# Hybrid attention block on one core: bias additions, norm chain, weight sums and last evictions at other places of the attention order

## The chip, the core and the metric

The kernel runs on one core of a Trainium2 chip. Five engines run their own in-order instruction queues: TensorE (PE; PEld are its weight loads), VectorE (DVE), ScalarE (ACT), GpSimd (POOL) and SyncE (SP), which here only issues DMAs. ACT issues DMAs too. They wait for one another by semaphores alone. The metric is the device time of one execution in microseconds; the median of several runs counts.

## The reference

All in float32, one layer, a sequence of 2048 tokens of width 1024:

```
h = rms_norm(x);  [q | k | v | p] = h @ w_in            (512 | 128 | 128 | 512 columns)
a = sliding_window_sink_attention(rms_norm(q), rms_norm(k), v)   8 heads, 2 KV heads, window 128
m = multiscale_pool(p)          trailing means over 2, 4, 8, 16 tokens minus the token, a map per group, bias, scale
x = x + concat([a, m]) @ w_out
x = x + (silu(gate) * val) @ w_down     gate | val = causal conv(3) of rms_norm(x) @ w_up, 2 * 2816 columns
```

## The kernel before

The sequence is cut into four blocks `a` of 512 tokens, each of four tiles of 128. A float32 product is made of three passes on PE over halves of the numbers: `passes` multiplies high by high, high by low and low by high (lines 1037 to 1039; a 128x512 matmul starts every 0.227 us). The high half of a weight is a copy on ACT (`split`, line 1419, into `w_hi`), the low half a subtraction on DVE (line 1899, into `w_lo`); halves once made for block 0 are kept in DRAM and brought back by SP (`bring`, lines 775 and 776). Weights move in units of 512 KB, through a ring of three; SP and the splits run two units (`LEAD`) ahead of PE.

The attention part, some 480 us, goes by one list, written out by hand in `attention_order()`: each entry is a step and a block. Every engine walks the same list (`walk`) and does its own share of each step, in that order; what it has no share in, it passes over. So the place of an entry orders an engine's own queue, and semaphores order the engines. Steps that the change touches, with their shares:

- `n1sq`, `n1sc` (a): norm of x. ACT squares four tiles, POOL takes the root, DVE multiplies by it (`n1sc`, line 1910, four instructions). `t1` then turns the tiles on PE (line 1109), with ACT making `hT_hi` and DVE `hT_lo` (line 1944) out of each bank; from the fifth tile on PE waits for the `hT_lo` that frees the bank.
- `pin` (a, g): the pooling projections, 24 long matmuls each; ACT carries them out of PSUM (lines 1486 to 1489), `win` on DVE makes the trailing sums (lines 1959, 1968).
- `q` (a, k): q's projection. In the last of four units ACT squares, DVE sums (2086), POOL takes the root (2505, 2507), DVE scales (2091), tile by tile.
- `s` (a, t): scores on PE (1214), two tiles to a pair of banks; DVE takes the maxima (2174), ACT the exponentials (1592). `inv` on DVE adds the sink to `row_sum` (line 2157, 128x8) and inverts it (2160); POOL multiplies the probabilities by it (2554). `sp`, `pt`, `av` spread, copy and multiply them by v.
- `o` (a, h, k) and, for blocks 1 and 2, `w`, `tp`, `tb`: the output projection; DVE adds the result to x (`r` or `n`; lines 2007 and 2023, the evictions). For blocks 1 and 2 it is a Winograd-like form with fewer products, on sums of weights made once in block 1: `to_load` (SP, lines 862, 863), `to_sum` (DVE, 2048), `to_hi` (ACT, 1579), `to_lo` (DVE, 2052), `to_store` (SP), j = 0 to 3.
- `bias_load`, `bias_sum`, `bias`: the folded bias, made once. `r_load` (SP, line 812) then brings x of block 0 into `r`, which `bias_sum` used. `rb` (b) adds the bias to block b's four tiles on POOL (line 2581); for blocks 0 and 1 it waits for each tile's last eviction.
- `n2sq`, `n2sc` (b): the second norm. ACT stores x2 by DMA (line 1638) and squares it (1440), after `rb`; DVE scales (1910) once all four stores have landed, since it writes over them; `t2` turns the tiles on PE (1337).

The mixer of block a-1 (`o`, `w`, `rb`, `n2sq`) runs inside the list's part for block a. Behind the attention part come the up-projection and the down-projection, on PE all the time.

Of the kernel before, what the change touches and what calls it, by code (L numbers as in the profile page):

```python
# [32 lines left out]
RAW, RING, LEAD, KEEP = 2, 3, 2, 4  # L33
# [3 lines left out]
def attention_order():  # L37
# [13 lines left out]
    for a in range(NB):  # L51
# [17 lines left out]
        units("q", a, (1,))  # L69
        if a == 1:  # L70
            units("r_load", a, ())
        if not more:
            units("rb", a - 1, ())
        units("win", a, (3,))
        if more:
            units("n1sc", a + 1, ())
        if a > 1:
            units("halves", a - 1, (2,))
        units("q", a, (2,))
        if a == 1:  # L80
            units("bias", a, ())
            units("to_sum", a, (0,))
        if not back:
# [42 lines left out]
        if a == 1:  # L126
            units("to_load", a, (0,))
            units("to_hi", a, (0,))
# [13 lines left out]
            units("o", a - 1, (1, 0))  # L142
            units("inv", a, (0,))
            units("o", a - 1, (1, 1))
            units("to_store", a, (0,))
            units("s", a, (2,), (3,))
            units("join", a, (0,), (1,))
            units("o", a - 1, (1, 2), (1, 3))
            units("to_store", a, (1,), (2,))
            units("inv", a, (1,))  # L150
        else:
# [28 lines left out]
            units("join", a, (1,))  # L180
            units("w", a - 1, (6, 1))
            units("inv", a, (1,))
        if more:
            units("rb", a - 1, ())
        if more:
# [5 lines left out]
            units("pin", a + 1, (0,))  # L191
            units("win", a + 1, (0,))
            if a == 1:
                units("to_sum", a, (3,))
            units("av", a, (0,), (1,))
            if a == 1:
                units("to_hi", a, (3,))
            units("n2sq", a - 1, ())
            units("pin", a + 1, (1,))
            if a == 1:  # L200
                units("to_load", a, (3,))
                units("to_lo", a, (3,))
            units("win", a + 1, (1,))
            units("n2sc", a - 1, ())
            units("sp", a, (2,), (3,))
# [46 lines left out]
UNIT = {}  # L252
# [184 lines left out]
def bass_hybrid_block(nc, x, norm1_g, w_in, q_norm_g, k_norm_g, attn_sinks, pool_w, pool_b, pool_scale,  # L437
# [20 lines left out]
    with ExitStack() as ctx:  # L458
# [576 lines left out]
        def _(pe):  # L1035
# [76 lines left out]
            def pin(a, n, g):  # L1112
# [12 lines left out]
                for i, k in enumerate(t1_order(a)):  # L1125
                    if g == 0 and i > (0, -1, 4, 4)[a]:
                        pe.wait_ge(S["hT_lo"], KT * a + i + 1)
                    if (a, g) == (1, 0) and i + 2 < KT:
                        turn_tile(a, i + 2)
                    c = slice(k * P, (k + 1) * P)  # L1130
                    mm = passes(ps[:, P_BANK + g, :], w_hi[:, w, c], w_lo[:, w, c], hT_hi[:, k, :], hT_lo[:, k, :],
                                i == 0, i == KT - 1)
# [70 lines left out]

            def s(a, t):
                pe.wait_ge(S["kT_ready"], a + 1)
                pe.wait_ge(S["qT_ready"], NT * a + (2, 4, 4, 4)[t])
# [683 lines left out]
        def _(dve):  # L1890
# [135 lines left out]
            def w(b, n, i, k):  # L2026
                if i == 6:
                    split(n + LEAD)
                if k == 1:
                    added(b, i, 0)  # L2030
                    added(b, i, 1)

            def swl(b, k):
# [62 lines left out]
            def q(a, n, k):  # L2096
                split(n + LEAD)
                if k < 3 or a == 0:
                    return
                for t in range(NT):  # L2100
                    summed(a, t)
                    if t == 2 and a - 1 in SEVEN:
                        split(UNIT["w", a - 1, 1, 0])
                    if t:
                        scaled(a, t - 1)
                if a - 1 in SEVEN:
                    split(UNIT["w", a - 1, 1, 1])
                scaled(a, NT - 1)
# [554 lines left out]
```

## Time and profile before

| | |
|---|---|
| runs, us | 1764.26 median of 3 (1764.02 to 1765.81) |
| the profiled execution, us | 1765.85; its span, first to last instruction, 1764.1 |
| busy us of the span | PE 1748.3, DVE 1340.5, ACT 822.2, POOL 302.0 |
| mean granted TensorE clock | 0.999 of full speed |
| DMA | 201 GB/s over the span |

The page tells busy time of each engine; a view of waits tells who stood idle and which engine's result ended it; a timeline lists one engine's instructions in order, in square brackets the idle time before one and what ended it. Ends of matmuls are modelled: of PE the distance between starts says more than a duration.

### The profile page before, as it was taken

Reading aid. Unit: us, or ns where it says so; the run is one execution under the profiler, and the core shown is the slowest. Engines: PE = TensorE matmul, PEld = TensorE weight load, DVE = VectorE, ACT = ScalarE, POOL = GpSimd, SP = SyncE. Lnnn points to the kernel's source line nnn. Section 1 sums busy time; section 2 is a strip of 40 time slices with the busy share of each in tenths; the row PEclk is TensorE's granted clock in tenths of the full one; section 3 lists DMA queues with packets and bytes.
Section 4 is the critical chain, followed back from the end, with each engine's and each line's share of the span. In section 5 each row is a group of like instructions: output and inputs, shape, how many; then the busy total and the mean of one; then the engine's idle time right before and its main releaser. Section 6 shows DMA issues by size and latency. Waiting matters only on the chain.

```text
span 1764.1 us, 23493 instructions
## 1 busy us (share of the span) xinstructions
PE 1748.3 (99%) x8454; PEld 1454.6 (82%) x8454; DVE 1340.5 (76%) x1773; ACT 822.2 (47%) x1448; POOL 302.0 (17%) x296
## 2 busy tenths in 40 slices
PE   8999999999999999999999999999999999999999
PEld 7787888888888888888888888888888888888887
DVE  4656856566789888889888878878877778865874
ACT  4565645535665444444454444444444433333321
POOL 2353312434110000000000000000004023220210
PEclk9999999999999999999999999999999999999999
DMA  8867688577747433332375232232237998976883
GB/s 325 282 226 281 237 323 297 206 286 263 252 154 259 136 95 120 132 95 72 132 279 174 84 96 72 84 91 77 79 95 242 345 354 316 306 254 222 293 287 131
DMA packets 224245, 355.30 MB, mean 201 GB/s; under 512 B 14650, under 2 KB 107010, under 8 KB 223106
## 3 DMA queue, kind: packets, MB, share of 16 engines
q1 hardware_dynamic: 204702, 301.31, 50.5%
q10 hardware_dynamic: 19427, 52.49, 7.6%
q8 instruction: 68, 1.11, 0.3%
q14 instruction: 48, 0.39, 0.1%
HBM read 273.00 MB, written 80.74 MB: 201 GB/s over the span
## 4 chain that ended last, share of the span: by engine, by line
PE 92%; DVE 3%; DMA 1%; ACT 1%; POOL 1%; issue 1%; SPq 0%; ACTq 0%; DVEq 0%
PE ps L1037 30%; PE ps L1039 29%; PE ps L1038 29%; DVE sums L1959 1%; PE ps L1214 1%; PE ps L1337 1%; POOL ss_q L2507 1%; PE ps L1238 1%; PE ps L1225 1%; DMA wP_d<-wp_kept 0%; DVE w_lo L1899 0%; PE ps L1109 0%; DMA raw<-in_w_in_dram 0%; DMA raw<-in_w_out_dram 0%; PE ps L1201 0%
## 5 line engine op out<-in xcount | busy, mean ns | idle before, releaser
L1037 PE MATMUL ps<-va_hi,wv 128*128 128x512 f32 x1232 | 479.4, 389 | 0.0
L1039 PE MATMUL ps<-va_hi,wv 128*128 128x512 f32 x1232 | 479.3, 389 | 0.0
L1038 PE MATMUL ps<-va_lo,wv 128*128 128x512 f32 x1232 | 479.3, 389 | 0.0
L1039 PEld LDWEIGHTS ps<-va_hi,wv 128*128 128x128 f32 x1232 | 231.3, 188 | 48.0
L1037 PEld LDWEIGHTS ps<-va_hi,wv 128*128 128x128 f32 x1232 | 231.3, 188 | 47.9
L1038 PEld LDWEIGHTS ps<-va_lo,wv 128*128 128x128 f32 x1232 | 231.3, 188 | 47.8
L1037 PE MATMUL ps<-dt_hi,ds_hi 128*128 128x512 f32 x616 | 239.6, 389 | 0.0
L1038 PE MATMUL ps<-dt_lo,ds_hi 128*128 128x512 f32 x616 | 239.6, 389 | 0.0
L1039 PE MATMUL ps<-dt_hi,ds_lo 128*128 128x512 f32 x616 | 239.6, 389 | 0.0
L2311 DVE SCALAR_TENSOR_TENSOR cb<-ub,cst,cb 128x1024 f32<-128x1024 f32 x176 | 217.8, 1279 | 8.3 <-ACT cb L1736 8.3
L1736 ACT ACTIVATE cb<-ub,cst 128x1024 f32<-128x1024 f32 x88 | 109.2, 1244 | 158.2 <-DVE ub L2360 94.5
L1853 ACT ACTIVATE ds_hi<-dts 128x512 fp32r<-128x512 f32 x110 | 69.5, 632 | 153.5 <-PE ps L1039 115.7
L1038 PEld LDWEIGHTS ps<-dt_lo,ds_hi 128*128 128x128 f32 x616 | 115.7, 188 | 24.1
L1037 PEld LDWEIGHTS ps<-dt_hi,ds_hi 128*128 128x128 f32 x616 | 115.7, 188 | 24.0
L1039 PEld LDWEIGHTS ps<-dt_hi,ds_lo 128*128 128x128 f32 x616 | 115.7, 188 | 23.9
L2631 POOL TENSOR_TENSOR dtw<-dw 128x512 f32<-128x512 f32 x55 | 86.7, 1578 | 276.9 <-DMA dw<-in_w_down_dram 250.0
L1688 ACT ACTIVATE wv<-tt 128x512 fp32r<-128x512 f32 x168 | 100.3, 623 | 65.2 <-PE ps L1039 40.3
L2464 DVE TENSOR_TENSOR ds_lo<-dts,ds_hi 128x512 fp32r<-128x512 f32 x110 | 91.4, 831 | 37.6 <-ACT ds_hi L1853 37.3
L2218 DVE TENSOR_TENSOR wv<-tt,wv 128x512 fp32r<-128x512 f32 x168 | 111.7, 686 | 4.0
L1688 ACT ACTIVATE wv<-rw 128x512 fp32r<-128x512 f32 x126 | 78.3, 623 | 57.7 <-DVE cb L2316 51.2
L2459 DVE TENSOR_TENSOR dts<-dg 128x512 f32<-128x512 f32 x110 | 80.1, 728 | 27.5 <-DMA dg<-gT_d 27.3
L1742 ACT ACTIVATE ub<-cb 128x1024 f32<-128x1024 f32 x44 | 46.8, 1063 | 98.8 <-DVE cb L2311 98.8
(223 smaller groups left out, 2894.0 us busy)
## 6 DMA issues: line engine op xcount, KB each, us to landing
dg<-gT_d SPq DMA_DIRECT2D x264, 256.0 KB, 5.4
rw<-in_w_up_dram SPq DMA_DIRECT2D x84, 512.0 KB, 5.2
dw<-in_w_down_dram SPq DMA_DIRECT2D x132, 256.0 KB, 5.5
gT_d<-cb ACTq DMA_DIRECT2D x44, 512.0 KB, 2.6
w_hi<-wA_d SPq DMA_DIRECT2D x30, 512.0 KB, 4.2
w_lo<-wA_d SPq DMA_DIRECT2D x30, 512.0 KB, 6.2
n<-in_x_dram SPq DMA_DIRECT2D x16, 512.0 KB, 8.6
raw<-in_w_out_dram SPq DMA_DIRECT2D x16, 512.0 KB, 5.0
```

What stands on the lines that cost most here:

```text
L1037: pe.matmul(out_ap, l_hi, r_hi, start=first, stop=False, skip_group_check=True)
L1038: pe.matmul(out_ap, l_hi, r_lo, start=False, stop=False, skip_group_check=True)
L1039: return pe.matmul(out_ap, l_lo, r_hi, start=False, stop=last, skip_group_check=True)
L1688: a_.activation(wv_hi[:, wslot(un, i), :], w_source(i), ACT.Copy).then_inc(S["u_hi"], 1)
L1736: a_.activation(cb[:, s, :], ub[:, s, 2:], ACT.Identity, bias=cbias[:, col], scale=cw[2][:, col]).then_inc(S[("tap2g", "tap2v")[s]], 1)
L1742: a_.activation(ub[:, 0, 2:], cb[:, 0, :], ACT.Silu).then_inc(S["silu"], 1)
L1853: a_.activation(ds_hi[:, sigma % SSLOTS, :], s_source(sigma), ACT.Copy).then_inc(S["s_hi"], 1)
L2218: v.tensor_tensor(wv_lo[:, w, :], w_source(i), as_f32(wv_hi[:, w, :]), ALU.subtract).then_inc(S["u_lo"], 1)
L2311: v.scalar_tensor_tensor(cb[:, s, :], ub[:, s, j:j + TS], cw[j][:, col], cb[:, s, :], ALU.mult, ALU.add).then_inc(S["conv"], 1)
L2459: v.tensor_tensor(s_source(sigma), dg[sigma % GRAW][:, 0, :], dg[sigma % GRAW][:, 1, :], ALU.subtract if minus else ALU.add).then_inc(S["s ...
L2464: v.tensor_tensor(ds_lo[:, sigma % SSLOTS, :], s_source(sigma), as_f32(ds_hi[:, sigma % SSLOTS, :]), ALU.subtract).then_inc(S["s_lo"], 1)
L2631: g_.tensor_tensor(t_source(tau), dw[:, tau % WRAW, 0, :], dw[:, tau % WRAW, 1, :], ALU.subtract if minus else ALU.add).then_inc(S["t_adde ...
```

## The change

Moves in the order (the first five points), and three edits in the programs of PE and DVE:

- `r_load(1)` goes from behind (q, 1, 1) to behind (q, 1, 3).
- `to_sum(1, 0)` goes ahead of (q, 1, 2), into the place of `n1sc(2)`, and `to_load(1, 0)` ahead of (q, 1, 3); `n1sc(2)` goes behind `inv(1, 0)`.
- `rb(0)` goes from behind `inv(1, 1)` to ahead of it, `rb(1)` likewise ahead of `inv(2, 1)`.
- In block 1, `to_sum(1, 3)` goes behind `av`, and `to_hi(1, 3)` behind `n2sq(0)`.
- `n2sc` goes ahead of `win(a+1, 1)`, in blocks 1 and 2, and in block 1 ahead of `to_lo(1, 3)`.
- PE: the scores (0, 3) are issued after two of the eight steps of unit (pin, 1, 3).
- DVE: in `w` the two evictions go ahead of the split; in `q` the split of (w, a-1, 1, 1) goes ahead of the third scaling.

```diff
--- before.py
+++ after.py
@@ -67,19 +67,19 @@
         if a > 1:
             units("halves", a - 1, (1,))
         units("q", a, (1,))
-        if a == 1:
-            units("r_load", a, ())
         if not more:
             units("rb", a - 1, ())
         units("win", a, (3,))
-        if more:
+        if a == 1:
+            units("to_sum", a, (0,))
+        elif more:
             units("n1sc", a + 1, ())
         if a > 1:
             units("halves", a - 1, (2,))
         units("q", a, (2,))
         if a == 1:
+            units("to_load", a, (0,))
             units("bias", a, ())
-            units("to_sum", a, (0,))
         if not back:
             units("wp", a, (0, 0))
         units("q", a, (3,))
@@ -124,7 +124,7 @@
             units("kve", a + 1, ())
             continue
         if a == 1:
-            units("to_load", a, (0,))
+            units("r_load", a, ())
             units("to_hi", a, (0,))
             units("o", a - 1, (0, 0), (0, 1))
             units("to_lo", a, (0,))
@@ -141,12 +141,14 @@
             units("to_lo", a, (1,), (2,))
             units("o", a - 1, (1, 0))
             units("inv", a, (0,))
+            units("n1sc", a + 1, ())
             units("o", a - 1, (1, 1))
             units("to_store", a, (0,))
             units("s", a, (2,), (3,))
             units("join", a, (0,), (1,))
             units("o", a - 1, (1, 2), (1, 3))
             units("to_store", a, (1,), (2,))
+            units("rb", a - 1, ())
             units("inv", a, (1,))
         else:
             units("w", a - 1, (0, 0), (0, 1), (1, 0))
@@ -179,9 +181,9 @@
             units("w", a - 1, (6, 0))
             units("join", a, (1,))
             units("w", a - 1, (6, 1))
+            if more:
+                units("rb", a - 1, ())
             units("inv", a, (1,))
-        if more:
-            units("rb", a - 1, ())
         if more:
             units("t1", a + 1, (0,))
             units("sp", a, (0,))
@@ -190,18 +192,18 @@
             units("pt", a, (0,), (1,))
             units("pin", a + 1, (0,))
             units("win", a + 1, (0,))
+            units("av", a, (0,), (1,))
+            units("n2sq", a - 1, ())
             if a == 1:
                 units("to_sum", a, (3,))
-            units("av", a, (0,), (1,))
-            if a == 1:
                 units("to_hi", a, (3,))
-            units("n2sq", a - 1, ())
             units("pin", a + 1, (1,))
             if a == 1:
                 units("to_load", a, (3,))
+            units("n2sc", a - 1, ())
+            if a == 1:
                 units("to_lo", a, (3,))
             units("win", a + 1, (1,))
-            units("n2sc", a - 1, ())
             units("sp", a, (2,), (3,))
             units("pt", a, (2,), (3,))
             units("pin", a + 1, (2,))
@@ -1125,6 +1127,8 @@
                 for i, k in enumerate(t1_order(a)):
                     if g == 0 and i > (0, -1, 4, 4)[a]:
                         pe.wait_ge(S["hT_lo"], KT * a + i + 1)
+                    if (a, g, i) == (1, 3, 2):
+                        scores(0, 3)
                     if (a, g) == (1, 0) and i + 2 < KT:
                         turn_tile(a, i + 2)
                     c = slice(k * P, (k + 1) * P)
@@ -1202,6 +1206,10 @@
                     mm.then_inc(S["qT_done"], 1)
 
             def s(a, t):
+                if (a, t) != (0, 3):
+                    scores(a, t)
+
+            def scores(a, t):
                 pe.wait_ge(S["kT_ready"], a + 1)
                 pe.wait_ge(S["qT_ready"], NT * a + (2, 4, 4, 4)[t])
                 if t >= 2:
@@ -2024,11 +2032,11 @@
                                 ).then_inc(S["out_added"], 1)
 
             def w(b, n, i, k):
-                if i == 6:
-                    split(n + LEAD)
                 if k == 1:
                     added(b, i, 0)
                     added(b, i, 1)
+                if i == 6:
+                    split(n + LEAD)
 
             def swl(b, k):
                 split(UNIT["w", b, 6, k])
@@ -2101,10 +2109,10 @@
                     summed(a, t)
                     if t == 2 and a - 1 in SEVEN:
                         split(UNIT["w", a - 1, 1, 0])
+                    if t == 3 and a - 1 in SEVEN:
+                        split(UNIT["w", a - 1, 1, 1])
                     if t:
                         scaled(a, t - 1)
-                if a - 1 in SEVEN:
-                    split(UNIT["w", a - 1, 1, 1])
                 scaled(a, NT - 1)
 
             def qn(a):
```

## Rows read from the trace of the kernel before

**Rows 1.** The page, its part 1: busy us, share of the span, instructions.
```profile
PE 1748.3 (99%) x8454; PEld 1454.6 (82%) x8454; DVE 1340.5 (76%) x1773; ACT 822.2 (47%) x1448; POOL 302.0 (17%) x296
```

**Rows 2.** PE's waits from 15 to 480 us: in total, times, longest.
```profile
PE ps L1337 <- DVE r L1910: 2.1, 1, 2.1
PE ps L1037 <- DVE w_lo L1899: 2.0, 2, 1.9
...
PE ps L1037 <- DVE n L2023: 0.5, 1, 0.5
PE ps L1214 <- ACT xs L1592: 0.5, 1, 0.5
PE ps L1225 <- DVE cat_lo L2195: 0.5, 1, 0.5
PE ps L1037 <- DMA w_lo<-wA_d: 0.4, 1, 0.4
```

**Rows 3.** Timeline of PE: start, us, line, out<-in, xcount [idle before <-releaser].
```profile
102.69 1.16 PE L1214 MATMUL ps<-kT,qT 64*128 64x128 f32 x16 [0.50 <-ACT xs L1592]
```

**Rows 4.** Timeline of SP's queue, 128 to 143 us.
```profile
128.89 0.43 SPq L812 DMA_DIRECT2D r<-in_x_dram  x1
```

**Rows 5.** DMA issues, KB, us to landing: from 128.87, 131.5 and 120.5 us.
```profile
r<-in_x_dram SPq DMA_DIRECT2D x1, 2048.0 KB, 11.2
...
w_lo<-wA_d SPq DMA_DIRECT2D x1, 512.0 KB, 10.9
...
wP_d<-wp_kept ACTq DMA_DIRECT2D x2, 256.0 KB, 6.5
```

**Rows 6.** Timeline of DVE, 149 to 169 us.
```profile
149.71 2.74 DVE L1910 TENSOR_SCALAR n<-n,rstd 128x1024 f32<-128x1024 f32 x4
...
156.27 1.22 DVE L1899 TENSOR_TENSOR w_lo<-raw,w_hi 128x1024 fp32r<-128x1024 f32 x1
157.41 1.27 DVE L2086 TENSOR_REDUCE ss_q<-xs 128x8 f32<-128x512 f32 x2
...
166.77 2.35 DVE L1899 TENSOR_TENSOR w_lo<-raw,w_hi 128x1024 fp32r<-128x1024 f32 x2
```

**Rows 7.** Timeline of PE at 168 us.
```profile
168.13 0.47 PE L1037 MATMUL ps<-w_hi,cat_hi 128*128 128x512 f32 x1 [1.85 <-DVE w_lo L1899]
```

**Rows 8.** Timeline of DVE, 192 to 213 us.
```profile
194.22 2.87 DVE L1899 TENSOR_TENSOR w_lo<-raw,w_hi 128x1024 fp32r<-128x1024 f32 x1
...
207.29 0.69 DVE L2007 TENSOR_TENSOR r<-ps,r 128x512 f32<-128x512 f32 x1 [0.67 <-PE ps L1039]
...
208.53 4.70 DVE L1944 SCALAR_TENSOR_TENSOR hT_lo<-ps,cst,hT_hi 128x512 fp32r<-128x512 f32 x7
```

**Rows 9.** Timeline of POOL, 193 to 222 us.
```profile
194.12 4.73 POOL L2554 TENSOR_TENSOR xs<-xs,row_sum 128x1024 f32<-128x1024 f32 x2 [27.99 <-DVE row_sum L2160]
208.37 3.76 POOL L2554 TENSOR_TENSOR xs<-xs,row_sum 128x1024 f32<-128x1024 f32 x2 [9.52 <-DVE row_sum L2160]
212.08 9.44 POOL L2581 TENSOR_TENSOR r<-r,bias_all 128x1024 f32<-128x1024 f32 x4
```

**Rows 10.** Timeline of DVE at 109 us and at 382 us.
```profile
109.83 0.95 DVE L2157 TENSOR_TENSOR row_sum<-row_sum,sink_exp 128x8 f32<-128x8 f32 x1 [1.05 <-ACT xs L1592]
...
381.79 5.60 DVE L1959 TENSOR_TENSOR sums<-sums 128x525 f32<-128x525 f32 x2
```

**Rows 11.** Timeline of PE at 210 us and at 238 us.
```profile
209.71 2.26 PE L1109 MATMUL ps<-ident,n 128*128 128x128 f32 x16
...
237.89 1.72 PE L1337 MATMUL ps<-ident,r 128*128 128x128 f32 x8 [2.06 <-DVE r L1910]
```

**Rows 12.** Windows: stretch, its us, busy (x) PE PEld DVE ACT POOL, clock, DMA.
```profile
239.00:240.00 1.00, 1.00 (x5) 0.90 (x4) 1.00 (x1) 0.83 (x2) 0.00 (x0) 0.50 1.03 422
```

**Rows 13.** Timeline of DVE at 329 us.
```profile
328.93 0.75 DVE L1944 SCALAR_TENSOR_TENSOR hT_lo<-ps,cst,hT_hi 128x512 fp32r<-128x512 f32 x1
```

**Rows 14.** Timeline of PE at 331 us.
```profile
330.70 1.95 PE L1109 MATMUL ps<-ident,n 128*128 128x128 f32 x16
```

## Prediction

> **What bounds the kernel now.** I read the page first. TensorE (PE) is busy in 99% of the span [rows 1], so no engine can be made faster to any use: all that is to be had, or lost, is the time in which PE stands still. The view of PE's waits from 15 to 480 us, the attention part, holds nearly all of it [rows 2]: 2.1 us for `n2sc` of block 0, 2.0 us (1.9 of it one wait) for a weight's low half `w_lo`, and four waits of about half a microsecond: for an exponential (ACT xs), for a DMA of `w_lo`, for `cat_lo`, and for an eviction into `n`. After 480 us PE shows no stall worth a line, so the change can move the end only by moving PE at these places or by making a new one. Most moves of this diff are on DVE, POOL and SP, each an in-order queue, so each has to be followed to the next thing that PE waits for. The timelines of these queues give the rest. Times below are positions in the trace of before.
>
> **1. Block 0's last scores.** PE has to wait 0.50 us before the scores of tile 3, at 102.69, until the exponentials of tile 1 have left the bank [rows 3]. With six of unit (pin, 1, 3)'s 24 matmuls between them (24 take 5.4 us, so six about 1.4) the wait is covered. With the restart it makes 0.7 us; one more change between small and long matmuls, there and back, takes an estimated 0.4 of it back (those around this row leave PE some 0.2 each). Gain 0.3 us (bounds 0 and 0.5). DVE sees tile 3's scores 0.7 us later, but ACT is still at tile 2's exponentials then.
>
> **2. r_load.** It issues 2 MB at 128.89, in front of the halves of unit (q, 1, 2), and takes 11.2 us to land; those halves take 10.9 us and PE stands 0.44 us for them [rows 2, 4, 5]. Behind the halves it is gone from their way: gain 0.65 us with PE's restart (bounds 0.5 and 0.7). What it is moved past matters too: it now stands on SP's queue just ahead of the loads of units (o, 0, 0, 0) and (o, 0, 0, 1), whose splits gate step 3.
>
> **3. Weight sums of block 1.** PE's 1.85 us stand before 168.13 ends with `w_lo` of (o, 0, 0, 2) [rows 7]. Read back on DVE [rows 6]: that split (166.77) comes after four rounds of q's norm chain, which began at 157.41; from that beginning to PE's restart are 10.7 us, all of them a chain. The chain began when DVE had done `n1sc` (2.74 us), a split, `to_sum` and the second split (1.22, at 156.27). Now `n1sc` is gone from there, and `to_sum` runs earlier, because `to_load` is issued before the load of (q, 1, 3). Then DVE is no longer last; the raw weights of (o, 0, 0, 1) are. `to_load` waits for the stores of wP_d: 6.5 us to land in a like place [rows 5], so about 138.2. Behind it on the queue come 1 MB of sums, 1 MB of halves, 2 MB of r and 1 MB of raw weights; at 1.35 us per 512 KB (the two halves of (q, 1, 2) land in the 2.7 us behind r: 131.91 + 10.9 against 128.89 + 11.2) the last lands 13.5 us on, and with some 1.5 us until the first moves at about 153, and with ACT's and DVE's halves of the split (1.1 and 1.2) the chain starts at 155.3 instead of 157.4. PE reaches that point 2.1 us earlier than before, steps 1 and 2 included. Bounds: 1.1 (the queue is a microsecond slower) and 2.9 (PE itself is late).
>
> **4. n1sc(2) behind inv(1, 0).** These four DVE instructions (2.74 us) now stand in front of the split of (o, 0, 1, 3), beside POOL's two multiplications at 194.12, 4.73 us for both, 1.9 each where nothing is beside them [rows 8, 9]. The split that stands there took 2.87 us where the same form takes 1.22 [rows 6, 8]: it waited for the first of them to end. The same is seen of a tiny addition (0.95 us instead of 0.16, beside a POOL multiplication) and of window sums beside POOL's bias additions (5.60 us for two that take 0.7 alone): DVE instructions with two SBUF inputs run only between two of POOL's [rows 10]. If `n1sc` waits likewise, its first runs when the first multiplication ends (196.0), the second after the second one (198.6), and the split ends at 201.7 instead of 197.1. If it doesn't, 200. No row shows a TENSOR_SCALAR behind POOL; I take the first, by the row at the very place [rows 8]. Everything of DVE up to the last evictions of o(0, 1) then moves by 4.2 us. The first of these, so far done at 204.97 and with room, ends at 209.1, the last at 211.0 instead of 208.0 [rows 8]. PE wants to turn block 2's tiles into those banks at 207.09 and waits 2 us.
> The Trainium skill (SBUF — State Buffer, Who interferes with whom) says that a `tensor_scalar` in a two-port mode and a GpSimd instruction block each other for the whole instruction, whoever comes first. By that rule `n1sc` waits, as I took it; without it the next step's 5.7 us would be 4.2.
>
> **5. rb(0) ahead of inv(1, 1).** This is the step that costs. The bias additions are 4 x 2.36 us on POOL (9.44, at 212.08) [rows 9]. They now start as soon as tile 0 is evicted, at 209.1, and DVE's `inv` stands right behind the last eviction. It holds two additions of row_sum, both inputs in SBUF, one after the other, with a reciprocal between. By [rows 10] the first waits for the end of the running bias addition (211.5), and, 0.3 us later, the second finds POOL's next one running and waits for its end (213.9). Behind it on DVE stands `hT_lo` of block 2, which began at 208.53 [rows 8] and now ends its first piece at 214.9; PE's second group of transposes (209.71, a tile per bank, each after a piece of `hT_lo`) starts there, and (pin, 2, 0) starts at 218.2 instead of 212.6 (the group's end, the second spread, then the pool unit) [rows 11]. Cost 5.7 us with step 4; 4.2 if `n1sc` doesn't wait. PE is idle for 2.5 us at a stretch in it. Of such a gap the trace has one case each way: after 1.85 us the clock stayed (168.13), after 2.06 us the granted clock was 0.50, the lower of its two levels (1.2 GHz), for some 3 us [rows 7, 11, 12]. I add 1.0 us here (bounds 0 and 1.6).
>
> **6. rb(1) ahead of inv(2, 1).** The same in block 2, without `n1sc`. rb starts at 327.05, after the 13th eviction; inv's additions are let in at 329.5 and 331.9, and `hT_lo` starts at 332.0 instead of 328.93 [rows 13]. PE's group at 330.70 waits for it: 2.9 us [rows 14]. Its gap is 2.0 us, between the two cases above: I add nothing, with 1.5 as the upper bound. That the muls behind rb end later (218 and 340 instead of 212 and 332) costs nothing: the probabilities are wanted 4 us and more after that.
>
> **7. n2sq, n2sc, to_sum(3), to_hi(3), win in block 1.** With rb 7 us earlier and ACT's squares ahead of `to_hi`, `n2sc` can run right after the stores of x2, and `win` after it. Counted from PE's start of (pin, 2, 0), the last store lands about 16.5 us on, `n2sc` is done at 19.4, and PE wants it at 22.3. So the wait of 2.06 us is gone, and the slow clock behind it (1.55 us: eight transposes in 1.72 us, the next matmuls at 0.43 instead of 0.23) [rows 11, 12]. `cat_lo` now precedes `to_sum`: its 0.46 us go too. With the restarts 4.4 us in all (bounds 3.5 and 4.8). Late next is `to_lo(3)` and block 1's `lefts`, with some microseconds of idle DVE behind them. For block 2 `n2sc` comes before `win`: `win` waits, nobody waits for it.
>
> **8. Last evictions of block 2 ahead of the split.** The wait of 0.54 us for `n` sits behind a split, 1.22 us in this form [rows 2, 6]. Gain 0.6 (0.5 to 0.7). The split of (w, a-1, 1, 1) one tile earlier: its ACT half is just ready then, nothing gained or lost.
>
> **Sum.** Gains 2.1 + 4.4 + 0.6 = 7.1; costs 5.7 + 1.0 + 2.9 = 9.6; together +2.5 us. The profiled execution took 1765.85 us, its span 1764.1; with the change 1768.35 and 1766.6. It is 1.6 above the median of the runs, 1764.26; the difference carries over: 1766.8 us. Changes under 0.2%, 3.5 us, are about what can't be told from none.
>
> **Rivals.**
> (a) POOL does not hold DVE's small additions up for long (both slip in at one boundary, or before the first bias addition has begun). Speaks for it: additions of 128x8 need the port for almost nothing. Against it: the addition of 0.95 us is of just this form, and a second instruction 0.03 us after the first found the port taken [rows 10]. If both slip in, step 5 costs 2 and step 6 0.6: 7.1 - 2.6 = 4.5 gained, 1759.8 us; if nothing waits, 7.1 gained, 1757.2.
> (b) Slower: the clock. If the idle stretches of steps 5 and 6 both bring the lower level, as the 2.06 us did, with 1.5 us each, and the SP queue leaves only 1.1 in step 3, then 6.1 gained and 5.7 + 2.9 + 3.0 lost: +5.5, 1769.8 us. It decides from a gap of between 1.85 and 2.06 us, and step 6's is 2.0.
> (c) r only changes what waits: the raw weights come behind it, step 3 gives nothing but steps 1 and 2, and (o, 0, 0, 0) itself is late; the rest as forecast: +3.6, 1767.9 us. It is an end of the forecast's range.
>
> **Chances.** Forecast with (c) 0.55, (a) 0.22, (b) 0.23. The forecast's own range is 1764 to 1769 (n1sc without waits -1.5, step 3 0.8 either way, the clock 1 either way); some 0.12 of it is over 3.5 us above before, 0.01 under. That gives faster 0.23, same 0.43, slower 0.34. The range for 8 in 10 is 1759.5 to 1770.5.
>
> **What would show it.** Steps 1, 2: no wait of PE <- ACT xs at 102, none <- DMA w_lo. Step 3: the wait for `w_lo` at 166 under a microsecond, its chain started by the landing of raw. Steps 4, 5: additions of row_sum of up to 2.4 us beside L2581, the transposes of L1109 in two parts with 2 us and more between, and a wait L1109 <- DVE hT_lo of about 2.5 us; the same in block 2 with 2 us. Step 7: no wait L1337 <- DVE r. If the additions of row_sum take 0.16 us as now, (a) holds and the forecast is wrong.

## The result, and the profile after

The changed kernel takes 1775.51 us (median of 6 runs, 1774.76 to 1777.95), the kernel before 1765.14 (6 runs, 1764.02 to 1767.16): a ratio of 1.006, 95% interval 1.0047 to 1.0073. It is slower by about 10.4 us; 1766.8 was predicted, with 1770.5 as the upper end. The profiled execution took 1775.70 us, its span 1773.9, against 1765.85 and 1764.1 before. Against the listing above, its lines stand two further down at `passes` (L1039 to L1041), `t1` (L1111) and in SP's program, and eight further down at `t2` (L1345), on ACT, DVE and POOL (`w_lo` L1907, `n1sc` and `n2sc` L1918, `row_sum` L2165, `rb` L2589).

PE's waits of the changed kernel from 15 to 480 us (in total, times, longest), to be read against [rows 2]:

```profile
PE ps L1111 <- DVE hT_lo L1952: 4.9, 3, 2.4
PE ps L1039 <- DMA w_lo<-wA_d: 3.6, 2, 3.1
PE ps L1039 <- DVE w_lo L1907: 2.2, 2, 1.4
PE ps L1111 <- DVE r L2015: 1.4, 1, 1.4
PE ps L1205 <- DVE xs L2099: 0.4, 1, 0.4
```

The waits that the change was to remove are gone (`n2sc`, ACT's `xs`, `cat_lo`, `n`, the DMA before 142), and that for `w_lo` before 168 has shrunk from 1.85 to 0.81. What stands there now is larger. The timeline of PE tells where, one line for each stall (start, us, instruction, [idle before <- what ended it]):

```profile
155.27 0.50 PE L1039 MATMUL ps<-w_hi,cat_hi 128*128 128x512 f32 x1 [1.41 <-DVE w_lo L1907]
...
167.70 0.47 PE L1039 MATMUL ps<-w_hi,cat_hi 128*128 128x512 f32 x1 [0.81 <-DVE w_lo L1907]
...
208.29 0.33 PE L1111 MATMUL ps<-ident,n 128*128 128x128 f32 x1 [1.43 <-DVE r L2015]
...
213.98 0.44 PE L1111 MATMUL ps<-ident,n 128*128 128x128 f32 x2 [2.37 <-DVE hT_lo L1952]
...
218.52 0.49 PE L1039 MATMUL ps<-hT_hi,w_hi 128*128 128x512 f32 x1
...
240.92 0.44 PE L1345 MATMUL ps<-ident,r 128*128 128x128 f32 x2
...
251.48 0.39 PE L1039 MATMUL ps<-w_hi,hT_hi 128*128 128x256 f32 x1 [3.10 <-DMA w_lo<-wA_d]
...
260.34 0.39 PE L1039 MATMUL ps<-w_hi,hT_hi 128*128 128x256 f32 x1 [0.47 <-DMA w_lo<-wA_d]
...
339.75 0.33 PE L1111 MATMUL ps<-ident,n 128*128 128x128 f32 x1 [1.87 <-DVE hT_lo L1952]
```

Behind three of the stalls stands a stretch at a lower granted clock, where the kernel before had one (windows: stretch, its us, busy (x) of PE, PEld, DVE, ACT, POOL, then PE's clock and DMA):

```profile
214.00:220.00 6.00, 6.00 (x30) 5.26 (x31) 4.67 (x7) 4.59 (x6) 6.00 (x4) 0.72 0.01 3
252.00:256.00 4.00, 4.00 (x23) 4.00 (x23) 1.21 (x1) 0.00 (x0) 0.00 (x0) 0.57 1.03 403
340.00:346.00 6.00, 6.00 (x31) 5.11 (x30) 4.36 (x7) 4.66 (x6) 6.00 (x4) 0.72 0.00 0
```

Six microseconds at a mean of 0.72 are 1.7 us lost, and so are four at 0.57. The kernel before had one such stretch, the one of [rows 12], with a mean of 0.57 over 238 to 242 us: 1.7 too. So the clock alone costs 5.1 us in this execution against 1.7 in that of before.

Following the same instruction of PE through both timelines gives the bill, beside what the prediction's steps had for that place:

| first matmul of | before, us | after, us | later by | predicted |
|---|---|---|---|---|
| (o, 0, 0, 0) | 154.80 | 155.27 | 0.5 | -0.95 |
| (o, 0, 0, 2) | 168.13 | 167.70 | -0.4 | -2.1 |
| (pin, 2, 0) | 212.59 | 218.52 | 5.9 | 4.6 |
| t2(0, 0) | 237.89 | 240.92 | 3.0 | 1.8 |
| (kv, 2, 0) | 246.71 | 251.48 | 4.8 | 0.2 |
| t1(3)'s second group | 330.70 | 339.75 | 9.1 | 3.1 |
| a common matmul at 478 us | 478.61 | 488.43 | 9.8 | 2.5 |

Two things the prediction did not have: at 168 PE is only 0.4 us ahead, not 2.1, and it loses 3.1 us at (kv, 2, 0). The reason for the second is on SP's queue (timeline of SP, and below it the landing of one of its issues, KB, us to landing):

```profile
239.24 0.32 SPq L870 DMA_DIRECT2D tO_d<-t_high  x1
239.60 0.43 SPq L870 DMA_DIRECT2D tO_d<-t_low  x1
240.13 1.84 SPq L777 DMA_DIRECT2D w_hi<-wA_d  x1
242.01 1.24 SPq L778 DMA_DIRECT2D w_lo<-wA_d  x1
243.30 4.26 SPq L783 DMA_DIRECT2D n<-in_x_dram  x4
```
```profile
w_lo<-wA_d SPq DMA_DIRECT2D x1, 512.0 KB, 9.4
```

`to_store(1, 3)`, the two issues at 239.24, waits on SP for DVE's `to_lo(3)`, and DVE now does that behind `n2sc`, which itself waits for the stores of x2 (timeline of DVE):

```profile
234.27 2.74 DVE L1918 TENSOR_SCALAR r<-r,rstd 128x1024 f32<-128x1024 f32 x4 [3.36 <-DMA x_d<-r]
236.93 2.28 DVE L2060 TENSOR_TENSOR t_low<-t_low,t_high 128x2048 fp32r<-128x2048 f32 x1
```

In the kernel before `to_lo(3)` ended at 229.9. Behind the store in SP's queue stand the halves of (kv, 2, 0), so these are issued 9 to 10 us later, land at 251.4 (242.01 + 9.4), and PE stands.

### The profile page after: what moved, and what is told of

It reads as the page before. It is cut to its first block, busy times and chain, and to the rows that moved or that the text cites. A ratio compares the mean times of both kernels' runs of the same rounds, so it can differ in the third digit from the quotient of the medians.

```text
span 1773.9 us, 23493 instructions
## 1 busy us (share of the span) xinstructions
PE 1753.1 (99%) x8454; PEld 1458.4 (82%) x8454; DVE 1339.2 (75%) x1773; ACT 822.2 (46%) x1448; POOL 299.1 (17%) x296
## 4 chain that ended last, share of the span: by engine, by line
PE 91%; DVE 3%; DMA 3%; ACT 1%; POOL 1%; SPq 1%; issue 1%; ACTq 0%; DVEq 0%
PE ps L1039 29%; PE ps L1041 29%; PE ps L1040 29%; DMA raw<-wP_d 1%; POOL ss_q L2515 1%; PE ps L1222 1%; PE ps L1246 1%; DMA w_lo<-wA_d 1%; PE ps L1233 1%; PE ps L1345 1%; DVE w_lo L1907 0%; PE ps L1111 0%; ACT w_hi L1427 0%; DVE row_sum L2165 0%; DVE n L1918 0%
## 5 line engine op out<-in xcount | busy, mean ns | idle before, releaser
L1039 PE MATMUL ps<-va_hi,wv 128*128 128x512 f32 x1232 | 479.8, 389 | 0.0
L1041 PE MATMUL ps<-va_hi,wv 128*128 128x512 f32 x1232 | 479.7, 389 | 0.0
L1041 PEld LDWEIGHTS ps<-va_hi,wv 128*128 128x128 f32 x1232 | 231.4, 188 | 48.0
L1039 PEld LDWEIGHTS ps<-va_hi,wv 128*128 128x128 f32 x1232 | 231.4, 188 | 47.8
L1039 PE MATMUL ps<-dt_hi,ds_hi 128*128 128x512 f32 x616 | 239.8, 389 | 0.0
L1041 PE MATMUL ps<-dt_hi,ds_lo 128*128 128x512 f32 x616 | 239.8, 389 | 0.0
L1039 PEld LDWEIGHTS ps<-dt_hi,ds_hi 128*128 128x128 f32 x616 | 115.7, 188 | 23.9
L1041 PEld LDWEIGHTS ps<-dt_hi,ds_lo 128*128 128x128 f32 x616 | 115.7, 188 | 23.8
L2639 POOL TENSOR_TENSOR dtw<-dw 128x512 f32<-128x512 f32 x55 | 82.3, 1498 | 281.1 <-DMA dw<-in_w_down_dram 261.7
```

Source lines behind the costliest of these rows:

```text
L1039: pe.matmul(out_ap, l_hi, r_hi, start=first, stop=False, skip_group_check=True)
L1041: return pe.matmul(out_ap, l_lo, r_hi, start=False, stop=last, skip_group_check=True)
L2639: g_.tensor_tensor(t_source(tau), dw[:, tau % WRAW, 0, :], dw[:, tau % WRAW, 1, :], ALU.subtract if minus else ALU.add).then_inc(S["t_adde ...
```

## The experiments

All medians stand beside runs of the kernel before on the same chip, whose medians were 1765.32 (first four), 1765.45 (next four) and 1765.07 (last four). Lines of a variant can stand one or two off those of the changed kernel.

**e1_store_late: SP's queue alone.**

```diff
             units("kv", a, (0,))
+            if a == 2:
+                units("to_store", 1, (3,))
...
             units("pin", a + 1, (3,))
-            if a == 1:
-                units("to_store", a, (3,))
```

> The changed kernel with one edit on SP's queue alone: to_store(1, 3) is issued behind the loads of unit (kv, 2, 0) and the four loads of x, no longer ahead of them. Theory (SP's queue): in the changed kernel SP stood until 239.2 us for to_lo(3), which now follows n2sc, and the halves of (kv, 2, 0) behind it landed at 251.4, so PE stood 3.1 us before 248 and 0.5 us before 259. With the edit both waits for a DMA of w_lo are gone, with the restarts 3.9 us: about 1771.6 us where the changed kernel takes 1775.5. Rival (the transfers themselves are slow there, or something else is late at the same place): the waits stay, or another of over a microsecond stands in their place, and the time stays within a microsecond of 1775.5 (or at about 1774).

1768.98 us, ratio 1.0023 (1.0015 to 1.0032). Both waits for the DMA are gone (its waits from 95 to 480 us):

```profile
PE ps L1111 <- DVE hT_lo L1952: 4.2, 2, 2.4
PE ps L1039 <- DVE w_lo L1907: 2.7, 2, 1.9
PE ps L1111 <- DVE r L2015: 1.5, 1, 1.5
PE ps L1111 <- DVE r L2031: 0.3, 1, 0.3
```

The theory of SP's queue holds. Between the two profiled executions PE gains 5.6 us of span: the 3.9 that was expected and the 1.7 of the slow stretch of 252 to 256 us, which went with the stall ahead of it. The medians differ by 6.5; the profiled execution of e1_store_late, 1770.07, is 1.1 above its median. More than half of the miss was this one queue. The next three runs build on this kernel.

**e2_rb_back: rb behind `inv` again, in both blocks.**

```diff
-            units("rb", a - 1, ())
             units("inv", a, (1,))
...
-            if more:
-                units("rb", a - 1, ())
             units("inv", a, (1,))
         if more:
+            units("rb", a - 1, ())
```

> The kernel of the run e1_store_late, and rb(0) and rb(1) back behind inv(1, 1) and inv(2, 1). Theory (DVE's additions of row_sum wait for POOL's bias additions): the additions take 0.16 us again, hT_lo starts about 2.5 us earlier, the waits for hT_lo of 2.4 us (at 211) and 1.9 us (at 337) are gone with their restarts and the low clock behind them: 3.3 us in block 1 and 2.4 in block 2, about 1766 us if the run before it takes 1771.6. The wait of 1.4 us for the evictions at 206 stays. Rival (rb late makes n2sc late): rb(0) then ends some 6 us later, PE waits for n2sc at 241 for up to 2 us, and block 1 gains 1.3 instead of 3.3: about 1768. Rival (the gap is of the evictions, not of rb): under 1 us in both blocks.

1762.67 us, 0.9985 (0.9977 to 0.9994): 6.3 less than e1_store_late, where 5.7 was expected. Both large waits for `hT_lo` are gone, and the clock is 1.00 from 15 to 480 us. PE's waits from 95 to 480 us:

```profile
PE ps L1037 <- DVE w_lo L1905: 2.6, 3, 1.5
PE ps L1109 <- DVE r L2013: 1.5, 1, 1.5
PE ps L1109 <- DVE r L2029: 0.3, 1, 0.3
```

Nothing of the rivals showed: `rb(0)` late holds nobody, since ACT reaches `n2sq` later still (it squares the first tile at 223.7, and POOL is done with all four at 224.0). With the additions in their present form, that `rb` comes first is all cost.

**e3_n1sc_back: n1sc(2) ahead of `to_sum(1, 0)`.**

```diff
-            units("n1sc", a + 1, ())
             units("o", a - 1, (1, 1))
...
+        if more:
+            units("n1sc", a + 1, ())
         if a == 1:
             units("to_sum", a, (0,))
-        elif more:
-            units("n1sc", a + 1, ())
```

> The kernel of the run e1_store_late, and n1sc(2) ahead of to_sum(1, 0), where DVE is idle from 149 to 154 us. Theory (n1sc beside POOL's multiplications holds up everything of DVE behind it by 4.2 us): the last evictions end at 206 instead of 210.0, PE's wait of 1.4 us for them is gone with its restart (1.6), rb starts 4 us earlier with them, so that hT_lo starts at 209 instead of 213.2 and the wait of 2.4 us for it shrinks to under 0.5 (with the low clock behind it 2.8 more): about 1767.2 if the run before takes 1771.6. n1sc itself costs nothing, since the split of (o, 0, 0, 0) waits for its weights until 154. Rival (PE only comes earlier to hT_lo's wait, which is set by rb's four additions and moves by less): 1.6 us gained and the wait for hT_lo stays at 2 us or more, about 1770.

1767.69 us, 1.0012 (1.0003 to 1.0021): 1.3 less. My theory, which had 4.4, falls, and the rival stands. The wait for the evictions is gone, but that for `hT_lo` grew from 2.37 to 3.11. The timeline of its DVE shows why:

```profile
207.69 1.88 DVE L2164 TENSOR_TENSOR row_sum<-row_sum,sink_exp 128x8 f32<-128x8 f32 x1
209.60 0.20 DVE L2167 RECIPROCAL row_sum<-row_sum 128x8 f32<-128x8 f32 x1
209.72 2.15 DVE L2164 TENSOR_TENSOR row_sum<-row_sum,sink_exp 128x8 f32<-128x8 f32 x1
```

`inv` comes 2.3 us earlier (207.69 against 209.95), but meets POOL's bias additions in another phase and waits 1.88 for the running one to end instead of 0.82. DVE's split of (o, 0, 1, 3) ends 4.0 us earlier than in the changed kernel (196.80 against 200.80), but the last evictions then wait for PE. Of these 4 us PE gets 1.3.

**e4_r_late: `r_load` behind the raw weights.**

```diff
-            units("r_load", a, ())
             units("to_hi", a, (0,))
             units("o", a - 1, (0, 0), (0, 1))
+            units("r_load", a, ())
```

> The kernel of the run e1_store_late, and r_load behind the loads of the raw weights of (o, 0, 0, 0) and (o, 0, 0, 1). Theory (the 2 MB of r stand in the way of the raw weights, which landed at 152.8): they land at about 149, both splits are done by 152, the wait of 1.4 us for w_lo before 153.5 is gone, and so is that of 0.8 us before 166.6, since q's norm chain begins as soon as q is squared: 2.5 us with the restarts, 1769.1 if the run before takes 1771.6. Rival (the clock of PE, or DVE, and not r): the wait before 153.5 goes, that before 166.6 stays because POOL's part of the chain (four rounds of 1.64 us) is as long as ever: 1.6 gained. Rival (POOL and the evictions behind set block 1 anyway): what is gained here is given back at the wait for the evictions at 206, which grows from 1.4 to up to 3.9 us: nothing gained.

1765.10 us, 0.9999 (0.999 to 1.0008): 3.9 less, where 2.5 was expected. In the profiles PE is 3.5 us ahead of e1_store_late's at the first turn of block 2's tiles (204.78 against 208.31): the wait before 153 was 1.88 us there, not the 1.41 of the changed kernel that the 2.5 was worked out from, and that for the evictions gave 0.6 more. The waits before 153 and 167 are both gone. The first rival (the one before 167 stays) falls; the third (all is given back at the evictions) too: that wait shrank, from 1.45 to 0.86. The landings of the issues around 140 us, of the changed kernel first and then of this one:

```profile
r<-in_x_dram SPq DMA_DIRECT2D x1, 2048.0 KB, 12.3
raw<-wP_d SPq DMA_DIRECT2D x2, 512.0 KB, 13.3
```
```profile
r<-in_x_dram SPq DMA_DIRECT2D x1, 2048.0 KB, 13.1
raw<-wP_d SPq DMA_DIRECT2D x2, 512.0 KB, 8.5
```

Nearly 5 us of the raw weights' way were the 2 MB of r, which nobody reads before the evictions at 179 (174.6 in e4_r_late).

**e5_reduce: the form of one DVE instruction, rb early** (on e1_store_late).

```diff
-        sink_exp = sb("sink_exp", [P, NT, 8])
+        both_sums = sb("both_sums", [P, NT, 2, 8])
+        exp_sum, sink_exp = both_sums[:, :, 0, :], both_sums[:, :, 1, :]
         row_sum = sb("row_sum", [P, NT, 8])
...
-                                       bias=shift[:, t, i:i + 1], accum_out=row_sum[:, t, i:i + 1])
+                                       bias=shift[:, t, i:i + 1], accum_out=exp_sum[:, t, i:i + 1])
...
-                v.tensor_tensor(row_sum[:, t, :], row_sum[:, t, :], sink_exp[:, t, :], ALU.add
+                v.tensor_reduce(row_sum[:, t, :], both_sums[:, t].rearrange("p s h -> p h s"), AX.X, ALU.add
```

> The kernel of the run e1_store_late (rb early in both blocks) with one DVE instruction in another form: the sum of row_sum and sink_exp is a tensor_reduce over two neighbouring fields of one tile (one input) instead of a tensor_tensor with two inputs in SBUF. The same is computed. Theory (a DVE instruction with two SBUF inputs runs only between two of POOL's, one with one input doesn't wait): the sums take under 0.3 us beside the bias additions, hT_lo starts at about 210.7 instead of 213.2, and the waits for hT_lo of 2.4 and 1.9 us are gone, with the low clock of 1.7 us behind each: about 1761 to 1762.5, what the run e2_rb_back took (1762.7), though rb stays early. Rival (any small DVE instruction between SBUF and SBUF, or rb's start itself, is what waits): the sums still take up to 2.2 us and the time stays at 1769.

1762.58 us, 0.9982 (0.9973 to 0.9991), within 0.1 of e2_rb_back. DVE's timeline, and the changed kernel's at the same place below it:

```profile
210.66 0.16 DVE L2166 TENSOR_REDUCE row_sum<-both_sums 128x8 f32<-128x16 f32 x1
210.86 0.20 DVE L2169 RECIPROCAL row_sum<-row_sum 128x8 f32<-128x8 f32 x1
210.98 0.12 DVE L2166 TENSOR_REDUCE row_sum<-both_sums 128x8 f32<-128x16 f32 x1
```
```profile
209.95 0.82 DVE L2165 TENSOR_TENSOR row_sum<-row_sum,sink_exp 128x8 f32<-128x8 f32 x1
210.80 0.20 DVE L2168 RECIPROCAL row_sum<-row_sum 128x8 f32<-128x8 f32 x1
210.92 2.15 DVE L2165 TENSOR_TENSOR row_sum<-row_sum,sink_exp 128x8 f32<-128x8 f32 x1
```

The two additions of 8 columns last 0.82 and 2.15 us beside `rb`; as reductions with one input they take 0.16 and 0.12 beside the same `rb`. The reciprocal, with one input, takes 0.20 in both kernels. `rb` runs at the same place in both (from 208.38 in the changed kernel, from 209.10 here), so the cause is the form of the two additions and not the place of `rb`. That it is the second SBUF input, and nothing else of the form, was not tried by itself. The Trainium skill (SBUF — State Buffer, Who interferes with whom) names this: an instruction with two SBUF inputs contends with a GpSimd instruction that reads SBUF, a `tensor_reduce` on trn2 never. The traces agree with both halves. One input is no guarantee, though: the TENSOR_SCALAR of `n1sc`, which reads one tensor and a scalar per partition, was held up too, as the next run shows.

**e6_n1sc_first: n1sc(2) ahead of inv(1, 0)** (on e2_rb_back).

```diff
-            units("inv", a, (0,))
             units("n1sc", a + 1, ())
+            units("inv", a, (0,))
```

> The kernel of the run e2_rb_back (1762.7 us) with n1sc(2) ahead of inv(1, 0) instead of behind it. Theory (n1sc waits for POOL's multiplications, which inv lets begin): n1sc takes 2.74 us instead of 4.2 more than that place gives it now (its first two took 2.34 and 2.38 us instead of 0.75), the last evictions end 1.5 to 3 us earlier, and the wait of 1.5 us for them at 206.9 shrinks to 0.2 or less: 1761.1. Rival (it is only the length of the four instructions that delays the evictions, wherever they stand): the wait stays at 1.3 or more, 1762.7. If inv(1, 0), now 2.7 us later, is late for someone, a new wait for the probabilities (L1231) stands in its place.

1761.49 us, 0.9977 (0.9968 to 0.9986): 1.2 less, and no wait for the evictions. The intervals of the two ratios overlap; that the wait of 1.5 us is gone is in the traces. Its DVE, then the changed kernel's:

```profile
193.26 2.73 DVE L1916 TENSOR_SCALAR n<-n,rstd 128x1024 f32<-128x1024 f32 x4
```
```profile
193.70 5.97 DVE L1918 TENSOR_SCALAR n<-n,rstd 128x1024 f32<-128x1024 f32 x4
```

The same four instructions take 2.73 us ahead of POOL's multiplications and 5.97 beside them.

**e7_all_rb and e8_all_reduce: the parts that stood the test, together.** The first is the changed kernel with the edits of e1, e2, e3 and e4; the second has the reduction of e5 in place of the edit of e2.

> The parts that stood the test, together: the changed kernel with to_store(1, 3) behind the loads of (kv, 2, 0), rb back, n1sc(2) ahead of to_sum(1, 0), r_load behind the raw weights of (o, 0, 0, 1). Theory (the four waits are independent): from the run e2_rb_back, 1762.7, the wait before 153 (1.66 with its restart), that before 167 (1.0) and that for the evictions at 207 (1.66) go: 4.3, about 1758.4, 0.4% under the kernel before. Rival (the waits stand in for one another: what is gained by 170 is given back at DVE's evictions or at hT_lo): the wait at 207 or a new one for hT_lo keeps 1 to 2 us: 1760.

1756.33 us, 0.9946 (0.9933 to 0.9958), 9 us under the kernel before and 2.1 under the 1758.4 that was expected. In the profiles 0.7 of that stands ahead of anything that differs from e2_rb_back (a wait of PE's ends at 86.81 against 87.52); the rest stays unexplained. From 95 to 480 us one wait is left in the view:

```profile
PE ps L1108 <- DVE r L2028: 0.3, 1, 0.3
```

> As the run e7_all_rb, but rb stays in its early place and the sum of row_sum is the reduction with one input (as in e5_reduce). If the reduction alone takes the wait away, the time is that of e7_all_rb within 1 us, 1758.4. Rival (rb early has a second cost: the multiplications with the inverse stand behind 9.4 us of bias additions on POOL, or POOL slows others): a wait of PE for the probabilities (the spread's transposes) or for hT_lo of 1 us or more, 1760 or above.

1757.33 us, 0.9953 (0.994 to 0.9965). In the profiles PE is already 1.6 us behind e7_all_rb at 88 us (88.42 against 86.81), ahead of anything that differs, 0.87 of it a wait for `w_lo` at 68. At 400 us, behind both early `rb`, it is 1.4 behind (399.82 against 398.39); after that comes one more wait for `w_lo`, 0.5 at 401. So `rb` early costs nothing measurable once the additions don't wait, and brings nothing either. Whether that explains the 1 us between the medians, no run shows.

**e9_step7_alone and e10_step7_store: the prediction's step 7 by itself, on the kernel before.** The first takes only the new order of block 1:

```diff
-            if a == 1:
-                units("to_sum", a, (3,))
             units("av", a, (0,), (1,))
+            units("n2sq", a - 1, ())
             if a == 1:
+                units("to_sum", a, (3,))
                 units("to_hi", a, (3,))
-            units("n2sq", a - 1, ())
...
+            units("n2sc", a - 1, ())
+            if a == 1:
                 units("to_lo", a, (3,))
             units("win", a + 1, (1,))
-            units("n2sc", a - 1, ())
```

> The kernel before with step 7 of the prediction alone: in block 1 n2sq, to_sum(3), to_hi(3), n2sc, to_lo(3) and win in the changed kernel's order, everything else as before. Theory (SP's queue): the waits of 2.06 and 0.46 us for n2sc and cat_lo and the low clock of 1.7 us go, 4.4 us; but to_lo(3) now ends at about 233.6 instead of 229.9 us, SP's to_store with it, and the halves of (kv, 2, 0) land some 12.2 us after it begins (as in the changed kernel, 239.24 to 251.44), at 245.9, where PE wants them at 242.2: a wait of about 3.6 us for a DMA of w_lo, with the low clock behind it or not. Together from 0.6 us faster to 1.1 slower than before: 1764.8 to 1766.5. Rival (the wait for the DMA in the changed kernel came from the steps ahead of it, which made block 1's end late for DVE): no wait or under 1 us here, 4.4 us gained, 1761.

1767.44 us, 1.0011 (1.0002 to 1.002), 0.9 over what I expected. SP's queue, and PE's stall:

```profile
234.65 0.32 SPq L868 DMA_DIRECT2D tO_d<-t_high  x1
```
```profile
246.46 0.39 PE L1037 MATMUL ps<-w_hi,hT_hi 128*128 128x256 f32 x1 [2.74 <-DMA w_lo<-wA_d]
```

The rival falls: the stall comes with step 7 alone, 2.74 us against 3.10, with a slow stretch at 247 to 250 behind it and a second stall of 0.67. The span of this execution is 2.0 us above that of before, but 1.3 of it stands ahead of the edit: a wait for a DMA before 144, 1.65 us here and 0.44 in the one of before. The second adds e1's edit on SP:

> The kernel of the run e9_step7_alone with to_store(1, 3) behind the loads of (kv, 2, 0), on SP alone. Theory: step 7 then gives what the prediction took it for, 4.4 us: 1761.0. Rival (the halves are late for another reason): as the run before it.

1761.34 us, 0.9981 (0.9972 to 0.999): step 7 then gives 3.7 us, near the 4.4 of the prediction. PE's waits for DMAs from 95 to 480 us, of e9_step7_alone and of this run:

```profile
PE ps L1037 <- DMA w_lo<-wA_d: 5.1, 3, 2.7
```
```profile
PE ps L1037 <- DMA w_lo<-wA_d: 0.6, 1, 0.6
```

By the medians step 7 on its own costs 2.4, and the place of one store in SP's queue is worth 6.1. By the traces it is worth 5.4: PE is 6.5 us ahead at 324 (324.11 against 330.64), but was 1.1 ahead already at 168 (168.29 against 169.39), before the edit.

**e11_e1_again and e12_e4_again: the clock.** Two kernels run once more, unchanged, one execution each (1768.45 and 1763.92 us).

> The kernel of the run e1_store_late once more, unchanged, for its granted clock alone. There the lower level (0.50) stood at 214 to 219 us, behind a stall of 2.37, and at 334 to 339 us, behind one of 1.87. Theory A (the stalls decide): the lower level stands at both places again. Theory B (it is chance, or where the chip happens to look): one of the two is missing, or the level falls at another stall, that of 1.9 us at 153.

Windows of the first run of e1_store_late, of PE's instruction behind the stall in the second, and of the windows of the second:

```profile
334.00:340.00 6.00, 5.69 (x29) 5.24 (x30) 5.09 (x8) 4.24 (x6) 6.00 (x4) 0.72 0.00 0
```
```profile
333.70 0.33 PE L1111 MATMUL ps<-ident,n 128*128 128x128 f32 x1 [1.87 <-DVE hT_lo L1952]
```
```profile
213.00:219.00 6.00, 5.18 (x28) 5.04 (x29) 5.65 (x9) 3.58 (x6) 6.00 (x3) 0.72 0.01 3
333.00:339.00 6.00, 5.30 (x33) 4.24 (x34) 5.25 (x9) 4.49 (x6) 6.00 (x3) 1.00 0.05 22
```

> The kernel of the run e4_r_late once more, unchanged, for its granted clock alone. There PE stood 2.37 us at 207.8 and 1.87 at 327.2, and the clock never fell below 1.00. Theory A (what PE did before decides, and it is the same in every execution): no lower level again. Theory B (chance): the level falls behind one of the two stalls, and the span is 1.7 us longer for it.

The span was 1762.1 us after 1762.3, and no stretch of it was slow, as in the first run. So both theories are right in part: the same kernel with the same stall of 1.87 us was followed by 0.50 once and by 1.00 once, while e4's two stalls left the clock alone in both profiled executions. Whether they always do isn't shown: of the 11 timed executions of e4_r_late, 8 have a mean granted clock of 0.999 or less, which one stretch that loses 1.7 us of 1764 would give, but these have no trace that says where (in e5_reduce one stands at 11 to 15 us).

## Why the prediction was wrong

**Step 7 failed, in the clause "Late next is `to_lo(3)` and block 1's `lefts`, with some microseconds of idle DVE behind them".** Its gain was right (t2(0, 0) moves from 5.9 to 3.0 us late, and the slow clock of 238 to 242 us is gone; `n2sc` was done 18.5 us after the start of (pin, 2, 0), forecast 19.4, though `rb` came 3.7 us earlier and not 7). But `to_lo(3)` has a reader that isn't on DVE: SP waits for it, with the next block's weights queued behind. The sentence asked what stands behind the late instruction on its own engine, not which in-order queue waits for it. Cost: 3.1 + 0.5 us of stall, restarts, and 1.7 us of clock, 5.6 in all, shown by e1, e9 and e10.

**Step 3 was mis-sized, and rival (c) was nearer here.** The lead at 168 was 0.4 us where 2.1 was predicted (bounds 1.1 to 2.9). The chain that the step leaned on is as long as it said (10.7 us from the start of the norm chain, 156.99, to PE's 167.70), and the raw weights landed at about 153, as it had it; but the chain was to start at 155.3, 1.7 us earlier. Between stands ACT (its timeline in the changed kernel):

```profile
152.90 1.06 ACT L1427 ACTIVATE w_hi<-raw 128x1024 fp32r<-128x1024 f32 x1 [9.53 <-DMA raw<-wP_d]
153.87 1.00 ACT L1531 ACTIVATE bias_all<-ps 128x1024 f32<-128x1024 f32 x1
154.77 1.05 ACT L1427 ACTIVATE w_hi<-raw 128x1024 fp32r<-128x1024 f32 x1
```

Behind r the weights of both units come late, so ACT had two splits and the copy of the bias to do after the landing, where the step had counted one split. That also holds PE at (o, 0, 0, 0) for 1.4 us, which [rows 7] could not show. e4 shows that r is the cause of both. Rival (c) named it ("(o, 0, 0, 0) itself is late") and priced it at 1767.9.

**Steps 4 and 5 had the mechanism right, and their sizes came out partly by luck.** The first two instructions of `n1sc` took 2.33 and 2.38 us and waited as the step took it from [rows 8]; the split behind them ended at 200.80, which with PE's lead of 0.5 there is the 4.2 us that was taken (the step's own 201.7 against 197.1 would be 4.6). The additions were let in at the ends of POOL's first and second bias addition. The prediction's times are positions in the trace of before; PE runs 0.4 us ahead of them here, so the end of the last evictions at 210.0 is to be read as 210.4 (predicted 211.0), and the start of (pin, 2, 0) at 218.52 as 218.9 (218.2, and 1.0 for the clock). From 168 to there PE lost 6.4 us, where 5.7 and 1.0 were predicted: 3.8 of waits and about 1.0 for restarts, together 0.9 less than the 5.7, and about 1.6 for the clock, 0.6 more than the 1.0 and the upper end of its bounds. That the two steps are not a sum of independent costs, e3 shows: freeing 4.0 us on DVE gave 1.3.

**Step 6: the stall was smaller, the clock dearer.** 1.87 us and its restart instead of 2.9, but the lower clock followed in this execution, 1.7 us; the bounds had 1.5 for it and the sum nothing. Together 3.7 against 2.9.

**Steps 1, 2 and 8 were right.** The wait at 102.69 is gone; the two more changes between small and long matmuls take some of it back, a net 0.3 us, as forecast. The wait before 142 is gone with r's move. `n` no longer waits at 446: 0.7.

Of the 7.3 us between the predicted 2.5 and the 9.8 us of the spans, SP's queue is 5.6, step 3 is 1.7 and step 6 is 0.8, together 8.1; a wait for `w_lo` at 407 us (0.18), not in the sum, went as well, and the 0.3 that steps 4 and 5 cost less and some tenths here and there make up the rest. Rival (a) was excluded by the additions of 0.82 and 2.15 us. Rival (b) had the direction and both slow stretches of steps 5 and 6, but not the size: SP's queue, with the third slow stretch, came from a stall it didn't know. Its rule, that the clock decides from a gap between 1.85 and 2.06 us, does not hold in the runs (below).

## What to carry to other kernels

When a step is put later, list every engine that waits for its result, and for each what is queued behind the waiting instruction; a DMA issuer that waits for a low-priority store holds up the urgent loads behind it, and moving the store behind them cost nothing here (e1, e10). A bulk load belongs behind the loads with a deadline, at the latest place that its own reader allows (e4). Beside a long GpSimd instruction on SBUF, a tiny VectorE addition with two SBUF inputs lasted as long as that instruction had still to run (0.82 to 2.15 us), and the same sum as a reduction with one input didn't (0.16, 0.12). Not every form with one tensor as input escapes: `n1sc` was held up as well (5.97 us instead of 2.73).

## What the hardware showed that I had not expected

The length of a stall alone does not decide whether the granted clock falls from 1.00 to 0.50. Every slow stretch that I summed cost the same, 1.7 us. Over the profiled executions, from 15 us on, all three stalls of 2.7 us or more were followed by one, and so was that of 2.06 [rows 11, 12]; of five of 2.37 us three were (these three had stood another 1.4 to 1.5 us some 6 us before, the two others 0.9), and of thirteen between 1.77 and 1.88 us three. The kernel of e1 had one behind its stall of 1.87 us in one execution and none in the next. The Trainium skill (TensorE: Matmul & The Clock Gate, Part 1: The HAM clock gate) says that the number of slow matmuls varies from run to run of one kernel; these two executions agree. The timed executions say the same. The kernel before, with its stall of 2.06 us, ran 74 times beside the experiments; in 22 of these its mean granted clock was 1.000, which leaves no room for a stretch of 1.7 us, so the one of [rows 12] that the prediction counted as certain is missing in about three of ten. Likewise 3 of 11 executions of e1_store_late have 1.000, though its stalls are of 2.37 and 1.87 us. What decides between equal stalls stays open.

A small instruction pays by when it comes, not by its length. `inv`'s first addition waited 0.82 us in the changed kernel and 1.88 in e3, where DVE came to it 2.3 us earlier.
